# A bias table written out 128 times and moved to GpSimd's queue, in a hybrid mixer and MoE block

## The chip, the cores and the metric

The kernel runs on one core of one Trainium2 chip. The metric is the device time of one execution in microseconds (us). All numbers of this kernel are 32-bit; matrices are multiplied in a split form (below) so that TensorE can take them in its fast 32-bit form.

## What is computed

One layer on 512 tokens of width 1024: a mixer of three branches, then a mixture of 16 experts, each with a residual. Shortened to what this case touches:

```python
def chunked_rel_attention(q, k, v, rel_bias):          # 8 heads of 64, chunks of 64
    scores = einsum('bcqhd,bckhd->bhcqk', q, k_band) * (A_HEAD_DIM ** -0.5)
    rel = clip(q_pos[:, None] - k_pos[None, :], -REL_CLIP, REL_CLIP) + REL_CLIP   # REL_CLIP = 128
    bias = rel_bias[:, rel]                             # rel_bias: 8 heads x 257
    scores = where(valid, scores + bias, -1e30)
    return einsum('bhcqk,bckhd->bcqhd', softmax(scores), v_band)

def reference(x, ...):
    xn = rms_norm(x, norm1_g)
    x = x + hybrid_mixer(xn, w_in, ..., w_branch, w_out)   # attention, spatial gating, linear recurrence
    xn = rms_norm(x, norm2_g)
    x = x + hierarchical_moe(xn, ..., w_gate, w_up, w_down)  # 16 experts, two per token
    return rms_norm(x, final_norm_g)
```

The bias of a query and a key depends on their distance alone, so the 128 x 256 bias tile of a head is a Toeplitz matrix: each row is the row above moved by one.

## The kernel before

It is written engine by engine, with semaphores by hand. Weights come in blocks of 512 KB (128 partitions x 1024 values), numbered b. A block goes through four hands in this order:

- SyncE (SP) loads block b into `raw` slot b % 4 (`load`, line 373). It first waits until block b - 4, the slot's last owner, has had its low part made.
- ScalarE (ACT) copies it to `w_hi` in the reduced form (`split_hi`, line 332), three blocks ahead of TensorE (`AHEAD = 3`), after block b - 4 has been multiplied.
- GpSimd (POOL) subtracts to get `w_lo` (`split_lo`, line 344) for all blocks of the mixer.
- TensorE (PE) multiplies hi by hi, hi by lo and lo by hi (`three`, lines 947 to 949). Before block b it waits for that block's low part (`lo_wait`).

Blocks 0 to 3 are the weights of the gating branch's second half (`B_SV`), 4 to 7 those of attention's v (`B_V`), from 8 on come the head pairs (`B_PAIR`), from 28 the gates, from 64 the output matrix. Then come the experts, 12 blocks each, with 24 buffers (`raw_a`, `raw_c`, `raw`, `raw_mg`, `macc`, `xn2T`) and the low parts made by VectorE.

At the start ACT squares the four row tiles of x, POOL takes the reciprocal root (line 530), VectorE (DVE) normalises a tile (line 1277), PE turns it (line 958), ACT writes `xn_hi` (line 653) and DVE `xn_lo` (`x_lo`, line 1267). In program order POOL then makes the low parts of blocks 0, 1, 2, clears `raw` slot 4 (line 535, semaphore `zero_done`, for which SP waits before it loads block 8), and goes on with block 3.

The bias: `rel_bias` is loaded into 8 partitions of `probs`, one per head. DVE repeats the last value 127 times behind the 257 (line 1256, early), ACT's queue stores the 8 rows of 384 values in the DRAM tensor `toep` (line 647, 12 KB), and SP's queue reads `toep` into `bias` (line 411): partition p takes 256 values from offset 1 + p, so all 128 partitions read overlapping pieces of the same 8 rows. The tile that arises is mirrored; DVE reads it backwards (`bias_and_max`, lines 1341 and 1343). POOL masks a corner of it (line 541) and the spatial weights (line 544) after the low part of block 8. The first reader of `bias` is the attention of the first head pair, after block 12.

Tiles are laid out in SBUF by hand with pads: `to_512` (96 values per partition) ahead of `raw`, `to_line` (8 values) ahead of `xT_hi`, and 5 values more than needed in `xrT`.

Of the kernel before, what the change touches and what calls it, by code (L numbers as in the profile page):

```python
# [22 lines left out]
F32 = mybir.dt.float32  # L23
# [3 lines left out]
ALU = mybir.AluOpType  # L27
ACT = mybir.ActivationFunctionType
AX = mybir.AxisListType

P = 128
TOK = 512
# [62 lines left out]
def build(nc, a, out):  # L95

    slots = nc.dram_tensor("slots", [SLOT_TILES * P, D], F32, kind="Internal").ap()
    toep = nc.dram_tensor("toep", [HEADS, 3 * P], F32, kind="Internal").ap()
# [7 lines left out]
    with ctx:  # L106
# [10 lines left out]
        sb(ctx, "to_512", [P, 96])  # L117
# [30 lines left out]
        with ExitStack() as s1:  # L148
# [14 lines left out]
            xrT = sb(s1, "xrT", [P, CONV + 4 + TOK])  # L163
# [6 lines left out]
            sb(s1, "pad_b1", [P, AREA_B - (NT * AW + 4 * P + 4 * P + AW + 2 * NPAIR * P + CONV + 4 + 7 * TOK)])  # L170
# [6 lines left out]
        with ExitStack() as s2:  # L177
# [15 lines left out]
            sb(s2, "to_line", [P, 8])  # L193
# [32 lines left out]
        def y_hi(t):  # L226
# [10 lines left out]
            "g1_in chan_in diag_in sgu_in relb_in toep_filled toep_out bias_in bias_done route_in g2_in "  # L237
# [126 lines left out]
        def _(sp):  # L364
# [43 lines left out]
            for kp in range(4):  # L408
                load(B_V + kp, rows2(w_in, 2 * kp, V0), 2)
            sp.wait_ge(S["toep_out"], 16)  # L410
            sp.dma_start(bias[:, :, :], bass.AP(toep.tensor, 1, [[1, P], [3 * P, HEADS], [1, 2 * P]]))\
              .then_inc(S["bias_in"], 16)
# [106 lines left out]
        def _(pool):  # L519
# [14 lines left out]

            pool.memset(gate_buf[:, 0:2, :], 0.0).then_inc(S["zero_done"], 1)
            for b in range(AHEAD, B_PAIR + AHEAD):
                split_lo(pool, b)
                if b == B_PAIR:

                    pool.wait_ge(S["bias_in"], 16)  # L540
                    pool.memset(bias[0:CHUNK, :, 0:CHUNK], NEG).then_inc(S["bias_done"], 1)
# [92 lines left out]
        def _(act):  # L634

            act.dma_start(g1_rows[:, :], a["norm1_g"][0:1, :].broadcast_to([P, D])).then_inc(S["g1_in"], 16)
            act.dma_start(probs[0:HEADS, 0, 0:2 * CLIP + 1], a["rel_bias"][0]).then_inc(S["relb_in"], 16)
# [7 lines left out]

            act.wait_ge(S["toep_filled"], 1)
            act.dma_start(toep, probs[0:HEADS, 0, 0:3 * P]).then_inc(S["toep_out"], 16)
# [69 lines left out]
            for j in range(NPAIR):  # L717
                for r in range(PER_PAIR):
# [6 lines left out]
                    if r == KK:  # L725

                        if j > 0:
                            act.wait_ge(S["conv_done"], j)
                        take(b - 1, xrT[:, CONV - 1:CONV - 1 + TOK], ACT.Copy)
# [513 lines left out]
        def _(dve):  # L1243
            chained = [0]

            def link(ins):
# [8 lines left out]
            dve.wait_ge(S["relb_in"], 16)  # L1255
            dve.tensor_copy(probs[0:HEADS, 0, 2 * CLIP + 1:3 * P],
                            probs[0:HEADS, 0, 2 * CLIP:2 * CLIP + 1].to_broadcast([HEADS, P - 1]))\
               .then_inc(S["toep_filled"], 1)
# [21 lines left out]
            for t in range(NT):  # L1280
                x_lo(t)

            dve.wait_ge(S["sguT_ps"], 1)
# [46 lines left out]
            def bias_and_max(n):  # L1330
# [9 lines left out]
                if w > near:  # L1340
                    link(dve.tensor_scalar(dst[:, 0:w - near], ps[:, 4 + buf, 0:w - near], DH ** -0.5,
                                           bias[:, h, 2 * P - 1:2 * P], ALU.mult, ALU.add))
# [408 lines left out]
```

## Time and profile before

| | us |
|---|---|
| median of 3 runs | 869.15 |
| lowest and highest | 867.15 and 870.6 |
| the profiled execution, whole | 869.15 |
| its span, first to last instruction | 867.4 |
| mean granted TensorE clock | 0.965 |
| PE busy | 801.0 |
| DVE, ACT, POOL busy | 495.5, 449.2, 218.0 |

The profiled execution's own time is also the median, so its durations can be used as they stand; 1.75 us of it lie outside the span. The rows are shown in a section of their own below: a row of a timeline is an instruction or a run of them, with its start, its length, and in brackets how long the engine stood idle before it and what ended that. A run of several (x3) starts with the first and ends with the last.

### The profile page before, as it was taken

The numbers are of one execution on the slowest core, as the hardware profiler recorded it, in microseconds if no ns is written. First come the engines' busy times: TensorE is split into PE (matmuls) and PEld (weight loads), VectorE is DVE, ScalarE is ACT, GpSimd is POOL, SyncE is SP. The second block draws the span as 40 slices with busy tenths as digits, with TensorE's granted clock in tenths as the row PEclk, the third lists the DMA queues.
The fourth block names the chain that finished last, engine by engine and source line by source line (L and its number), as shares of the span: only waits on it lengthen the run. The fifth ranks groups of instructions, "written<-read, shape, count | busy, mean of one in ns | idle before, by whom it ended". The sixth has DMA issues, their size and how long they took to land.

```text
span 867.4 us, 10612 instructions
## 1 busy us (share of the span) xinstructions
PE 801.0 (92%) x3635; PEld 631.7 (73%) x3635; DVE 495.5 (57%) x649; ACT 449.2 (52%) x580; POOL 218.0 (25%) x126
## 2 busy tenths in 40 slices
PE   4999999999979999999999967899999999999960
PEld 3887766676756888888888866688787787877750
DVE  6613647657472222204012435698889898988865
ACT  5244637454552232323222221687888878887842
POOL 5554323132232344444444234000000000000013
PEclk9999999999999999999999967999999999999995
DMA  8665451512120343333328364999999999975945
GB/s 308 179 243 188 128 194 49 194 49 74 40 80 27 89 169 118 99 93 95 98 96 280 131 239 197 366 400 385 405 389 393 408 395 406 389 299 209 367 137 207
DMA packets 126633, 186.76 MB, mean 215 GB/s; under 512 B 9149, under 2 KB 61957, under 8 KB 126597
## 3 DMA queue, kind: packets, MB, share of 16 engines
q1 hardware_dynamic: 119156, 167.82, 54.3%
q10 hardware_dynamic: 5136, 10.08, 3.1%
q0 software_dynamic: 2304, 8.39, 2.7%
q8 instruction: 22, 0.36, 0.2%
q14 instruction: 15, 0.11, 0.0%
HBM read 158.99 MB, written 27.28 MB: 215 GB/s over the span
## 4 chain that ended last, share of the span: by engine, by line
PE 81%; DVE 7%; ACT 4%; issue 3%; DMA 2%; POOL 1%; ACTq 1%; DVEq 0%; SPq 0%
PE ps L947 24%; PE ps L949 23%; PE ps L948 23%; PE ps L1030 3%; PE ps L1010 2%; PE ps L1171 2%; PE ps L1019 1%; DVE w_lo L350 1%; PE ps L1119 1%; ACT w_hi L339 1%; DVE rgate L1394 1%; PE ps L1178 1%; DMA x<-in_x 1%; ACT xn L879 1%; DMA slots<-y_tile 1%
## 5 line engine op out<-in xcount | busy, mean ns | idle before, releaser
L344 POOL TENSOR_TENSOR w_lo<-raw,w_hi 128x1024 fp32r<-128x1024 f32 x72 | 176.2, 2450 | 286.8 <-ACT w_hi L332 286.8
L332 ACT ACTIVATE w_hi<-raw 128x1024 fp32r<-128x1024 f32 x73 | 77.0, 1057 | 169.0 <-PE ps L949 159.9
L947 PE MATMUL ps<-xn_hi,w_hi 128*128 128x512 f32 x352 | 143.8, 409 | 0.0
L949 PE MATMUL ps<-xn_hi,w_lo 128*128 128x512 f32 x352 | 137.5, 390 | 0.0
L948 PE MATMUL ps<-xn_lo,w_hi 128*128 128x512 f32 x352 | 137.3, 390 | 0.0
L947 PE MATMUL ps<-w_hi,xT_hi 128*128 128x512 f32 x256 | 105.2, 411 | 8.1 <-DVE xT_lo L1644 5.5
L948 PE MATMUL ps<-w_lo,xT_hi 128*128 128x512 f32 x256 | 102.3, 399 | 0.0
L949 PE MATMUL ps<-w_hi,xT_lo 128*128 128x512 f32 x256 | 102.2, 399 | 0.0
L947 PEld LDWEIGHTS ps<-xn_hi,w_hi 128*128 128x128 f32 x352 | 66.0, 188 | 26.8 <-issue 13.8
L614 POOL DMA_INDIRECT raw_mg<-slots,slot_idx x7 | 6.9, 982 | 303.6 <-ACTq L930 295.1
L949 PEld LDWEIGHTS ps<-xn_hi,w_lo 128*128 128x128 f32 x352 | 66.1, 188 | 14.4
L948 PEld LDWEIGHTS ps<-xn_lo,w_hi 128*128 128x128 f32 x352 | 66.2, 188 | 13.1 <-issue 1.0
L350 DVE TENSOR_TENSOR w_lo<-raw_mg,w_hi 128x1024 fp32r<-128x1024 f32 x57 | 68.0, 1221 | 4.3 <-ACT w_hi L339 1.7
L947 PEld LDWEIGHTS ps<-w_hi,xT_hi 128*128 128x128 f32 x256 | 48.9, 191 | 24.2 <-DVE w_lo L350 8.0
L1457 DVE SCALAR_TENSOR_TENSOR macc<-raw,ps 128x512 f32<-128x512 f32 x16 | 11.0, 688 | 96.5 <-PE ps L949 96.3
L339 ACT ACTIVATE w_hi<-raw_mg 128x1024 fp32r<-128x1024 f32 x57 | 59.7, 1056 | 11.3 <-PE ps L949 11.3
L350 DVE TENSOR_TENSOR w_lo<-raw,w_hi 128x1024 fp32r<-128x1024 f32 x43 | 51.3, 1220 | 14.6 <-ACT w_hi L339 14.6
L949 PEld LDWEIGHTS ps<-w_hi,xT_lo 128*128 128x128 f32 x256 | 48.9, 191 | 11.7
L948 PEld LDWEIGHTS ps<-w_lo,xT_hi 128*128 128x128 f32 x256 | 48.9, 191 | 10.4
L947 PE MATMUL ps<-w_hi,hT_hi 128*128 128x512 f32 x128 | 51.8, 405 | 2.9 <-DVE hT_lo L1651 2.9
L339 ACT ACTIVATE w_hi<-raw 128x1024 fp32r<-128x1024 f32 x43 | 44.0, 1055 | 16.1 <-PE ps L949 16.1
L949 PE MATMUL ps<-w_hi,hT_lo 128*128 128x512 f32 x128 | 50.5, 395 | 0.0
(260 smaller groups left out, 1457.5 us busy)
## 6 DMA issues: line engine op xcount, KB each, us to landing
raw<-in_w_in SPq DMA_DIRECT2D x52, 512.0 KB, 3.7
raw_mg<-in_exp_w_down SPq DMA_DIRECT2D x36, 512.0 KB, 8.3
raw<-in_exp_w_gate SPq DMA_DIRECT2D x28, 512.0 KB, 10.3
raw_a<-in_exp_w_gate SPq DMA_DIRECT2D x27, 512.0 KB, 9.8
raw_c<-in_exp_w_up SPq DMA_DIRECT2D x27, 512.0 KB, 9.2
slots<-raw SPq DMA_DIRECT2D x24, 512.0 KB, 6.5
raw_mg<-in_exp_w_up SPq DMA_DIRECT2D x21, 512.0 KB, 9.8
raw<-in_exp_w_up SPq DMA_DIRECT2D x16, 512.0 KB, 9.5
```

The source lines that it names most:

```text
L332: nc.scalar.activation(w_hi[:, b % HI_SLOTS, :], raw_buf(b), ACT.Copy)\
L339: nc.scalar.activation(w_hi[:, (8 + r) % HI_SLOTS, :], buf, ACT.Copy).then_inc(S["hi_act"], 1)
L344: eng.tensor_tensor(w_lo[:, b % HI_SLOTS, :], raw_buf(b), w_hi[:, b % HI_SLOTS, :].bitcast(F32), ALU.subtract)\
L350: eng.tensor_tensor(w_lo[:, (8 + r) % HI_SLOTS, :], place(at, r)[0], w_hi[:, (8 + r) % HI_SLOTS, :].bitcast(F32), ALU.subtract)\
L879: act.activation(at.y, ps[:, 5:7, :].rearrange("p a n -> p (a n)"), ACT.Copy).then_inc(S["y_act"], 1)
L947: pe.matmul(dst, hi_l, hi_r, start=start, stop=False)
L948: pe.matmul(dst, hi_l, lo_r, start=False, stop=False)
L949: return pe.matmul(dst, lo_l, hi_r, start=False, stop=stop)
L1010: pe.matmul(ps[:, 4 + n % 2, 0:(i + 1) * P], qT[hp, jp % 2, i * P:(i + 1) * P], kT[hp, jp % 2, 0:(i + 1) * P], start=True, stop=True).then ...
L1030: mm = pe.matmul(ps[DH * h:DH * (h + 1), 7, i * P:(i + 1) * P], v_rows[:, kt, (2 * jp + h) * DH:(2 * jp + h + 1) * DH], probsT[:, kt * P:( ...
L1171: mm = pe.transpose(ps[:, 3 + k // 4, (k % 4) * P:(k % 4 + 1) * P], rows[:, k * P:(k + 1) * P], ident[:, :])
L1457: dve.scalar_tensor_tensor(out=macc[:, 1, :], in0=gate_buf[:, g % 3, :], scalar=1.0, in1=ps[:, 2 + c, :], op0=ALU.add, op1=ALU.mult)\
```

## The change

- `toep` grows from 8 x 384 to 8 x 128 x 384 values: every head's row is stored 128 times, one copy per partition (1.57 MB instead of 12 KB). Each partition then reads its 256 values out of its own copy, from offset 127 - p, so that the tile arrives the right way round.
- `rel_bias` is loaded next to the row that is built; DVE writes the row in two copies, the repeated value first, and the 257 values reversed. This stands behind the four `x_lo` now, not ahead of the normalisation, and the load of `bias` is not issued by SP, nor the store of `toep` by ACT: POOL issues both, after the low part of block 2, and waits for the first to land before the second.
- POOL waits for `bias` and masks after block 4, not block 8.
- DVE makes `xn_lo` of tile 0 behind the normalisation of tile 2 and that of tile 1 behind that of tile 3, not all four at the end.
- The pads `to_512` and `to_line` go, and `xrT` is 515 values, not 520. Since tiles begin at multiples of 32 bytes, `xrT` still takes as much room as before.

GpSimd's program from the reciprocal roots on, before (`w_lo` are the low parts of blocks 0, 1, ...; `raw` the cleared slot):

```order
L530 TENSOR_TENSOR stat<-stat,minus_half 128x1 [waits x0_stat] x3
L344 TENSOR_TENSOR w_lo<-raw,w_hi 128x1024 [waits hi_act] x3
L535 MEMSET raw 128x1024
L344 TENSOR_TENSOR w_lo<-raw,w_hi 128x1024 [waits hi_act] x6
L541 MEMSET bias 64x8x64 [waits bias_in]
L544 AFFINE_SELECT sgu_wT<-sgu_wT 128x512 [waits sguT_done]
```

The same place in the changed kernel:

```order
L525 TENSOR_TENSOR stat<-stat,minus_half 128x1 [waits x0_stat] x3
L342 TENSOR_TENSOR w_lo<-raw,w_hi 128x1024 [waits hi_act] x3
L532 DMA toep<-probs 1024x1x384 [waits toep_rev]
L534 DMA bias<-toep 128x8x256 [waits toep_out]
L537 MEMSET raw 128x1024
L342 TENSOR_TENSOR w_lo<-raw,w_hi 128x1024 [waits hi_act] x2
L543 MEMSET bias 64x8x64 [waits bias_in]
L546 AFFINE_SELECT sgu_wT<-sgu_wT 128x512 [waits sguT_done]
```

Two DMAs, each with a wait, now stand between the low parts of blocks 2 and 3, and the wait for `bias` stands after two more low parts, not six.

VectorE's program at the start, before (`x` is the row tile that is normalised, `probs` holds the bias row):

```order
L1256 COPY probs<-probs 8x127 [waits relb_in]
L1262 TENSOR_SCALAR stat<-stat 128x1 [waits x0_sq_done,g1_in]
L1262 TENSOR_SCALAR stat<-stat 128x1 [waits x0_sq_done]
L1277 SCALAR_TENSOR_TENSOR x<-x,stat,g_rows 128x1024 [waits x0_rstd]
L1262 TENSOR_SCALAR stat<-stat 128x1 [waits x0_sq_done]
L1277 SCALAR_TENSOR_TENSOR x<-x,stat,g_rows 128x1024 [waits x0_rstd]
L1262 TENSOR_SCALAR stat<-stat 128x1 [waits x0_sq_done]
L1277 SCALAR_TENSOR_TENSOR x<-x,stat,g_rows 128x1024 [waits x0_rstd] x2
L1267 TENSOR_TENSOR xn_lo<-ps,xn_hi 128x8x128 [waits xn_hi_done] x4
L1284 COPY par<-ps 128x56 [waits sguT_ps]
```

and in the changed kernel, from the normalisation of tile 1 on:

```order
L1257 TENSOR_SCALAR stat<-stat 128x1 [waits x0_sq_done]
L1272 SCALAR_TENSOR_TENSOR x<-x,stat,g_rows 128x1024 [waits x0_rstd]
L1257 TENSOR_SCALAR stat<-stat 128x1 [waits x0_sq_done]
L1272 SCALAR_TENSOR_TENSOR x<-x,stat,g_rows 128x1024 [waits x0_rstd]
L1262 TENSOR_TENSOR xn_lo<-ps,xn_hi 128x8x128 [waits xn_hi_done]
L1272 SCALAR_TENSOR_TENSOR x<-x,stat,g_rows 128x1024 [waits x0_rstd]
L1262 TENSOR_TENSOR xn_lo<-ps,xn_hi 128x8x128 [waits xn_hi_done] x3
L1281 COPY probs<-probs 8x127 [waits relb_in]
L1284 COPY probs<-probs 8x257
L1287 COPY par<-ps 128x56 [waits sguT_ps]
```

The copy that fills the bias row went from ahead of the normalisation to behind the last `xn_lo`, and one `xn_lo` went ahead of the last normalised tile. On SyncE's queue the load of `bias` between block 7 and block 8 is gone; the rest stands as it was.

The diff, without the renaming of `toep_filled` to `toep_rev` in the list of semaphores:

```diff
-    toep = nc.dram_tensor("toep", [HEADS, 3 * P], F32, kind="Internal").ap()
+    toep = nc.dram_tensor("toep", [HEADS, P, 3 * P], F32, kind="Internal").ap()
...
-        sb(ctx, "to_512", [P, 96])
...
-            xrT = sb(s1, "xrT", [P, CONV + 4 + TOK])
+            xrT = sb(s1, "xrT", [P, CONV - 1 + TOK])
...
-            sb(s2, "to_line", [P, 8])
... SyncE
-            sp.wait_ge(S["toep_out"], 16)
-            sp.dma_start(bias[:, :, :], bass.AP(toep.tensor, 1, [[1, P], [3 * P, HEADS], [1, 2 * P]]))\
-              .then_inc(S["bias_in"], 16)
... GpSimd
+            pool.wait_ge(S["toep_rev"], 2)
+            pool.dma_start(toep, probs[0:HEADS, 0, 0:3 * P].unsqueeze(1).to_broadcast([HEADS, P, 3 * P])).then_inc(S["toep_out"], 16)
+            pool.wait_ge(S["toep_out"], 16)
+            pool.dma_start(bias[:, :, :], bass.AP(toep.tensor, P - 1, [[3 * P - 1, P], [3 * P * P, HEADS], [1, 2 * P]]))\
+                .then_inc(S["bias_in"], 16)
+
             pool.memset(gate_buf[:, 0:2, :], 0.0).then_inc(S["zero_done"], 1)
             for b in range(AHEAD, B_PAIR + AHEAD):
                 split_lo(pool, b)
-                if b == B_PAIR:
+                if b == AHEAD + 1:
                     pool.wait_ge(S["bias_in"], 16)
-                    pool.memset(bias[0:CHUNK, :, 0:CHUNK], NEG).then_inc(S["bias_done"], 1)
+                    pool.memset(bias[0:CHUNK, :, 3 * CHUNK:4 * CHUNK], NEG).then_inc(S["bias_done"], 1)
... ScalarE
-            act.dma_start(probs[0:HEADS, 0, 0:2 * CLIP + 1], a["rel_bias"][0]).then_inc(S["relb_in"], 16)
+            act.dma_start(probs[0:HEADS, 1, 0:2 * CLIP + 1], a["rel_bias"][0]).then_inc(S["relb_in"], 16)
...
-            act.wait_ge(S["toep_filled"], 1)
-            act.dma_start(toep, probs[0:HEADS, 0, 0:3 * P]).then_inc(S["toep_out"], 16)
... VectorE
-            dve.wait_ge(S["relb_in"], 16)
-            dve.tensor_copy(probs[0:HEADS, 0, 2 * CLIP + 1:3 * P],
-                            probs[0:HEADS, 0, 2 * CLIP:2 * CLIP + 1].to_broadcast([HEADS, P - 1]))\
-               .then_inc(S["toep_filled"], 1)
...
                    .then_inc(S["x0_norm"], 1)
-            for t in range(NT):
+                if t >= 2:
+                    x_lo(t - 2)
+            for t in range(NT - 2, NT):
                 x_lo(t)
+            dve.wait_ge(S["relb_in"], 16)
+            dve.tensor_copy(probs[0:HEADS, 0, 0:P - 1],
+                            probs[0:HEADS, 1, 2 * CLIP:2 * CLIP + 1].to_broadcast([HEADS, P - 1]))\
+               .then_inc(S["toep_rev"], 1)
+            dve.tensor_copy(probs[0:HEADS, 0, P - 1:3 * P], probs[0:HEADS, 1, 2 * CLIP::-1])\
+               .then_inc(S["toep_rev"], 1)
...
-                                           bias[:, h, 2 * P - 1:2 * P], ALU.mult, ALU.add))
+                                           bias[:, h, 0:1], ALU.mult, ALU.add))
...
-                                              scalar=DH ** -0.5, in1=bias[:, h, near - 1::-1],
+                                              scalar=DH ** -0.5, in1=bias[:, h, 2 * P - near:],
```

## Rows read from the trace of the kernel before

**Rows 1.** The page: engines, granted clock in 40 slices, chain by engine

```profile
PE 801.0 (92%) x3635; PEld 631.7 (73%) x3635; DVE 495.5 (57%) x649; ACT 449.2 (52%) x580; POOL 218.0 (25%) x126
PEclk9999999999999999999999967999999999999995
PE 81%; DVE 7%; ACT 4%; issue 3%; DMA 2%; POOL 1%; ACTq 1%; DVEq 0%; SPq 0%
```

**Rows 2.** Waits of PE, whole span: us in total, times, longest

```profile
PE ps L958 <- DVE x L1277: 12.2, 2, 10.3
...
PE ps L947 <- POOL w_lo L344: 3.0, 1, 3.0
```

**Rows 3.** Timeline of POOL, 7 to 36 us: start, length, engine, line, operation

```profile
12.03 1.52 POOL L530 TENSOR_TENSOR stat<-stat,minus_half 128x1 f32<-128x1 f32 x1 [0.95 <-DVE stat L1262]
13.52 8.05 POOL L344 TENSOR_TENSOR w_lo<-raw,w_hi 128x1024 fp32r<-128x1024 f32 x3
21.51 0.96 POOL L535 MEMSET raw<- 128x1024 f32 x1
27.25 7.12 POOL L344 TENSOR_TENSOR w_lo<-raw,w_hi 128x1024 fp32r<-128x1024 f32 x3 [4.78 <-ACT w_hi L332]
```

**Rows 4.** Timeline of DVE, first 25 us

```profile
6.20 0.21 DVE L1256 COPY probs<-probs 8x127 f32<-8x127 f32 x1 [4.12 <-DMA probs<-in_rel_bias]
...
13.59 3.38 DVE L1277 SCALAR_TENSOR_TENSOR x<-x,stat,g_rows 128x1024 f32<-128x1024 f32 x1 [0.44 <-POOL stat L530]
16.89 4.61 DVE L1267 TENSOR_TENSOR xn_lo<-ps,xn_hi 128x1024 fp32r<-128x1024 f32 x4
```

**Rows 5.** Timeline of PE, 17 to 36 us: last turned tile, block 0, start of block 3

```profile
17.02 1.09 PE L958 MATMUL ps<-ident,x 128*128 128x128 f32 x8 [1.85 <-DVE x L1277]
18.25 0.47 PE L947 MATMUL ps<-w_hi,xn_hi 128*128 128x512 f32 x1
...
35.23 0.39 PE L949 MATMUL ps<-w_hi,xn_lo 128*128 128x512 f32 x1
35.46 0.39 PE L947 MATMUL ps<-w_hi,xn_hi 128*128 128x512 f32 x1
```

**Rows 6.** Timeline of ACT and SyncE's queue, 30 to 50 us

```profile
46.60 1.06 ACT L332 ACTIVATE w_hi<-raw 128x1024 fp32r<-128x1024 f32 x1 [2.47 <-PE ps L949]
...
32.10 18.43 SPq L373 DMA_DIRECT2D raw<-in_w_in  x5
```

**Rows 7.** DMA issues: KB each, median us to landing; then the GpSimd-issued kind

```profile
raw_a<-in_exp_w_gate SPq DMA_DIRECT2D x27, 512.0 KB, 9.8
raw_c<-in_exp_w_up SPq DMA_DIRECT2D x27, 512.0 KB, 9.2
...
out<-raw_mg SPq DMA_DIRECT2D x4, 512.0 KB, 2.6
...
bias<-toep SPq DMA_DIRECT2D x1, 1024.0 KB, 6.4
...
L587 POOL DMA_INDIRECT slots<-xn,slot_idx x8 | 7.9, 986 | 13.3 <-DVE slot_idx L1614 11.1 <-issue 2.1
```

**Rows 8.** Busy time by stretch; last three numbers granted clock, DMA share, GB/s

```profile
8.00:12.00 4.00, 1.70 (x8) 1.63 (x9) 2.85 (x6) 3.66 (x7) 2.28 (x3) 1.00 1.04 409
...
24.00:28.00 4.00, 4.00 (x21) 3.34 (x22) 2.73 (x10) 1.99 (x3) 0.76 (x1) 1.00 0.17 62
...
600.00:700.00 100.00, 99.10 (x459) 79.74 (x458) 88.57 (x83) 80.70 (x88) 0.00 (x0) 1.00 1.04 400
```

**Rows 9.** Timeline of PE after two gaps, and the stretch when the clock returns

```profile
257.85 0.77 PE L947 MATMUL ps<-br_hi,w_hi 128*128 128x512 f32 x1 [2.97 <-POOL w_lo L344]
258.41 0.63 PE L948 MATMUL ps<-br_lo,w_hi 128*128 128x512 f32 x1
...
258.84 0.63 PE L949 MATMUL ps<-br_hi,w_lo 128*128 128x512 f32 x1
...
263.00:264.00 1.00, 1.00 (x6) 0.77 (x6) 0.00 (x0) 0.00 (x0) 0.00 (x0) 0.65 0.00 0
...
536.82 0.80 PE L947 MATMUL ps<-w_hi,xT_hi 128*128 128x512 f32 x1 [2.68 <-DVE xT_lo L1644]
```

**Rows 10.** Waits of SyncE's queue, 540 to 830 us, and the chain's tile pitch

```profile
SPq L377 <- DVE w_lo L350: 93.0, 108, 2.9
...
603.46 0.87 PE ps L1171 x8
...
640.36 0.87 PE ps L1171 x8
```

**Rows 11.** Readers of bias: duration ns min/median/max, first and last start

```profile
L1343 DVE SCALAR_TENSOR_TENSOR probs<-ps,bias x22: 276/424/426, 96.8 to 271.6; 128x256 f32<-128x256 f32 x16, 128x128 f32<-128x128 f32 x6
L1341 DVE TENSOR_SCALAR probs<-ps,bias x11: 345/471/485, 103.9 to 271.1; 128x256 f32<-128x256 f32 x6, 128x128 f32<-128x128 f32 x5
```

More of the change, by code:

```diff
@@ L169, in build @@
             gu = sb(s1, "gu", [P, TOK])
-            sb(s1, "pad_b1", [P, AREA_B - (NT * AW + 4 * P + 4 * P + AW + 2 * NPAIR * P + CONV + 4 + 7 * TOK)])
+            sb(s1, "pad_b1", [P, AREA_B - (NT * AW + 4 * P + 4 * P + AW + 2 * NPAIR * P + CONV - 1 + 7 * TOK)])
             br_hi = sb(s1, "br_hi", [P, 3, NPAIR, TOK], F32R)
@@ L236, in build @@
             "ident_done consts_pool consts_dve zero_done zeros_stored "
-            "g1_in chan_in diag_in sgu_in relb_in toep_filled toep_out bias_in bias_done route_in g2_in "
+            "g1_in chan_in diag_in sgu_in relb_in toep_rev toep_out bias_in bias_done route_in g2_in "
             "sgu_raw sguT_ps sguT_done mask_done sv_sq sv_stat sv_rstd sv_done sp_exp sp_done halved "
@@ L728, in _ @@
                             act.wait_ge(S["conv_done"], j)
-                        take(b - 1, xrT[:, CONV - 1:CONV - 1 + TOK], ACT.Copy)
+                        take(b - 1, xrT[:, CONV - 1:], ACT.Copy)
                     if r == QQ:
```

## The prediction, as put on record

> **What bounds the kernel now.** I read the page's first lines, then PE's waits, then the timelines of the first 50 us, since the change lives there. The page shows PE busy for 801.0 of 867.4 us, its clock at the full level in nearly all slices, and 81% of the chain on PE [rows 1]. PE's longest wait is for the first normalised tile, 12.2 us in two pieces; for POOL's low parts it waits once, 3.0 us [rows 2]. From 18.25 us on PE runs block after block without a gap: a matmul starts every 0.23 us, and block 3 begins at 35.46 [rows 5]. So anything that holds PE in this stretch is added to the end in full, and anything taken from another engine here is worth nothing. The number to watch is the margin of block 3's low part: POOL makes those of blocks 3, 4, 5 from 27.25 on, 7.12 us for three, the first done near 29.6 [rows 3]. PE needs it at 35.46. The margin is 5.8 us.
>
> **The store and the load on POOL.** This is the heavy edit. Of block 3 onward every low part is POOL's, and two DMAs with two waits now stand ahead of it. The sum runs along POOL:
>
> - Start. The third low part ends at 21.5 [rows 3]. VectorE must first write the reversed row: its four xn_lo end at 21.5 before [rows 4]. In the change the first comes earlier, so the last ends near 20.4 (16.97 + 3 x 1.15). The first copy took 0.21 [rows 4]; the second, 257 values from SBUF, is at most the 0.42 of a 256-value read of `bias` [rows 11]. DVE's last normalisation took 3.38 us beside POOL's low part, where the rest of that form take about 1.3, so I let the copies start only as POOL stops: ready at 21.5 + 0.6 = 22.1.
> - X, from issue to landing of the store: 8 x 128 x 1536 bytes = 1.57 MB. No row shows a large transfer out of 8 partitions. Low end: the full rate of 409 GB/s [rows 8] gives 3.9 us, and 1.3 us on top, which is what the 2.6 us of a 512 KB store [rows 7] leaves over its 1.3 us at that rate: 5.2. High end: a full transfer takes 1/16 of its bytes from 8 partitions; were that share their limit, 25.6 GB/s, it would be 61.5 + 1.3 = 62.8. I take twice that share, 51 GB/s: 30.8 + 1.3 = 32.1. It is a choice nearer the high end, since all rows I have at high rates spread over 128 partitions and here a single row of 1.5 KB is read 128 times over. Little else is on the queues: 62 GB/s from 24 to 28 us [rows 8].
> - G, the time that POOL itself spends on issuing the second DMA (1024 pieces of 1 KB). A GpSimd-issued DMA of 128 pieces keeps POOL for 0.99 us [rows 7]. Low end: the same, 1.0. High end: eight times that, 7.9. I take the middle, 4.4. The first DMA's issue overlaps its own transfer and lies inside X.
> - Then the clearing of `raw`, 0.96, and the low part, 2.40 (7.12 / 3) [rows 3].
>
> Block 3's low part is ready at 22.1 + X + G + 3.4 = 25.5 + X + G, and PE stands still for X + G - 10.0 us. With 32.1 + 4.4 that is **26.5 us**. With both low ends it is negative (-3.8): hidden. With both high ends 60.7.
>
> The Trainium skill has a price where no row does: "SBUF — State Buffer", section on the DMA port swizzle, gives 27.6 GB/s for a transfer over partitions 0 to 3 and about 27 GB/s per port; 0 to 7 reach two ports. By that page the store would take an estimated 29 us and about 2 more, and the wait of PE would be about 25. No run here shows it.
>
> **What starts again after the gap.** After 2.97 us without work PE's matmuls came 0.43 us apart, not 0.23, the clock at 1.2 GHz, from 257.85 until inside 263 to 264 [rows 8, 9]: 12 matmuls x 0.2 = 2.4, with the small ones 2.9. After the 2.68 us gap at 536.82 [rows 9] it was eight matmuls, 1.6. I take 2.3. POOL then needs 2.4 us per block and PE 5.4, so the other low parts do not delay PE again. POOL's wait for `bias` stands after block 4's: the load took 6.4 from issue [rows 7], and G + 0.96 + 2 x 2.40 cover all but a fraction; block 5 is wanted 10.9 us after block 3. SyncE's loads wait for low parts: block 7's goes out after block 3's part, block 8's after block 4's and `zero_done`. Before, block 8's load went at 32.10 and its high part was made at 46.60, when PE let it [rows 6]; the 14 us between stay, as both ends move together.
>
> **Small edits.** `xn_lo` of tile 0 came 16.89 to 18.05, and PE began block 0 at 18.25, 0.14 after the last turned tile (17.02 + 1.09) [rows 4, 5]. With tile 0's part made before, at most 0.2 us is gained; the last normalisation waits for POOL's low part until 15.7 anyway and does not move. I count -0.1. SyncE and ACT lose one DMA issue each; neither is waited for there. DVE's read of `bias` forwards in place of backwards: 424 ns for 256 columns and 276 for 128 is 1.16 ns per column backwards, the forward form beside it 485 and 345, 1.09 [rows 11]: at most 0.02 us each in 32 readers, nothing.
>
> **The pads.** All tiles move down by 384 bytes, and those behind `router_b` and from `br_hi` on start 32 bytes past a multiple of 64. Two places could feel it. The expert loads: `raw_a`, `raw` and `raw_mg` go from multiples of 256 bytes to 128 past one, where `raw_c` stood before; it landed in 9.2 us, `raw_a` in 9.8 [rows 7], so this offset showed no price. Were the transfers some per cent slower, the demand of 400 GB/s against the best of 409 [rows 8] would no longer be met, but two tiles take 36.9 us [rows 10] and the buffers hold two tiles: a load landing in 10 us has 26 us to spare, and SyncE's queue waits 93.0 us in all for buffers [rows 10], not buffers for it. I count 0. PE reading `xn_hi`, `xn_lo` and `br_*` at the new offset: no row shows it at this rate; between 0 and, as an estimate, one line more in 32 on 0.23 us for the mixer's some 1500 matmuls, 11 us. I take 0, because PE's pace was the same for all tiles before.
>
> **Sum.** 26.5 + 2.3 - 0.1 = +28.7 on the span of 867.4, so 896.1, and with the 1.75 us outside it **897.9 us**. The profiled execution, 869.15, is also the median, so nothing is corrected.
>
> **Rivals.**
>
> - *The store is limited by engines, not by the partitions.* Eight source rows may keep half the 16 DMA engines busy: 204 GB/s, 7.7 + 1.3 = 9.0 us. For it: a load of 1024 pieces out of eight rows, `bias` itself, landed 1 MB in 6.4 us [rows 7]. Against: that read DRAM, not 8 partitions. PE waits 9.0 + 4.4 - 10.0 = 3.4, and with the clock's 1.6 to 2.9 the time is 874.6; with the first issue taking 7.9 before the transfer and G at 7.9, 886. The Trainium skill, "DMA: Bandwidth & Descriptors", on how many engines a DMA uses, has a rule that gives 8 here, as the largest number up to 16 that divides both slowest dimensions, 8 and 1024. Chance 0.22.
> - *Hidden: not slower.* The store and the second issue together stay under 10.0 us, which is where this decides; X of 5.2 with G of up to 4.8 does it. The margin swallows both, and the time is 869.1. For it: a 512 KB store landed in 2.6. Against: it needs the full rate from 8 partitions. Chance 0.07.
> - *One share only.* X near 62.8: PE waits 57.2, the time is 928.6. Chance 0.07.
> - *The offsets cost too.* The forecast's wait plus up to 11 us of slower matmuls or loads: 903 to 909. It decides if PE's spacing leaves 0.227 in blocks 0 to 2. Chance 0.07.
>
> **How the numbers follow.** The forecast has the rest, 0.57, with its own range from 885 (X of 20, G of 4) to 912 (X of 42, G of 7.9). A gain of over 0.5% would need 4.3 us, and nothing in the change is worth more than 0.2: 0.02. A measurement of this kernel can tell about 0.5% from no change. Within 0.5% (864.8 to 873.5) lie the hidden case and the shortest of the eight-engine case: 0.10. Slower: 0.88. The range reaches from 873 to 915 and leaves out the one-share case, the hidden one and little else.
>
> **What would show it.** On POOL between the third and the fourth low part: one DMA, a wait of X for `toep` (32 us forecast, 9 in the first rival), a second DMA of G, the clearing, and a PE gap before block 3 equal to X + G - 10.0, with matmuls 0.43 us apart behind it. The bytes per us over the wait tell 51 from 204 GB/s. The expert stage should take the same time as before, and blocks 0 to 2 the same spacing. The prediction is wrong if PE has no gap at block 3, if the gap is there but a later wait was absorbed by it, or if the time is lost behind 100 us.

## The result, and the profile after

The changed kernel is slower: its median is 904.01 us against 869.88 us of the kernel before, run beside it on the same chip, a ratio of 1.0396 with the interval [1.0359, 1.0433]. The span of the profiled execution grew from 867.4 to 900.3 us, by 32.9; by the medians the whole time grew by 34.1. The forecast was 897.9 us.

The page of the changed kernel, with its line of busy times, the granted clock in 40 slices and the chain by engine (to be held against [rows 1]):

```profile
PE 811.4 (90%) x3635; PEld 631.8 (70%) x3635; DVE 488.2 (54%) x650; ACT 449.1 (50%) x580; POOL 220.1 (24%) x128
...
PEclk9859999999999999999999995999999999999995
...
PE 78%; DVE 6%; DMA 6%; ACT 4%; issue 3%; POOL 1%; ACTq 1%; SPq 0%; DVEq 0%
```

Two things are to be seen. DMA's share of the chain went from 2% to 6%. And PE, whose work is the same, is busy for 10.4 us longer. PE's waits of the changed kernel (against [rows 2]):

```profile
PE ps L946 <- POOL w_lo L342: 27.6, 2, 24.7
```

GpSimd's timeline of the changed kernel at the place of [rows 3]:

```profile
13.57 8.07 POOL L342 TENSOR_TENSOR w_lo<-raw,w_hi 128x1024 fp32r<-128x1024 f32 x3
22.23 1.34 POOL L532 DMA_DIRECT2D toep<-probs  x1 [0.59 <-DVE probs L1284]
56.13 0.98 POOL L534 DMA_DIRECT2D bias<-toep  x1 [32.56 <-DMA toep<-probs]
57.10 0.97 POOL L537 MEMSET raw<- 128x1024 f32 x1
58.02 4.66 POOL L342 TENSOR_TENSOR w_lo<-raw,w_hi 128x1024 fp32r<-128x1024 f32 x2
```

The store goes out at 22.23, GpSimd stands for 32.56 us until it has landed, issues the load in 0.98, and only then clears `raw` and makes block 3's low part. The two DMAs, issue to landing, and the rate from 26 to 56 us (last number of the row, GB/s; the third last is the granted clock):

```profile
toep<-probs POOLq DMA_DIRECT2D x1, 1536.0 KB, 33.6
...
bias<-toep POOLq DMA_DIRECT2D x1, 1024.0 KB, 6.1
```

```profile
26.00:56.00 30.00, 9.76 (x42) 7.52 (x40) 4.66 (x29) 4.06 (x5) 0.00 (x0) 0.72 0.47 50
```

TensorE's timeline of the changed kernel at block 3:

```profile
60.42 0.80 PE L946 MATMUL ps<-w_hi,xn_hi 128*128 128x512 f32 x1 [24.66 <-POOL w_lo L342]
61.01 0.63 PE L947 MATMUL ps<-w_lo,xn_hi 128*128 128x512 f32 x1
...
66.13 0.52 PE L947 MATMUL ps<-w_lo,xn_hi 128*128 128x512 f32 x1
66.49 0.39 PE L948 MATMUL ps<-w_hi,xn_lo 128*128 128x512 f32 x1
```

It idles for 24.66 us, and the matmuls behind the gap come 0.43 us apart, the pace at 1.2 GHz, until 66.13: 13 of them, 13 x 0.2 = 2.6 us. That explains 24.6 (27.6 - 3.0) + 2.6 = 27.2 of the 32.9 us. The remaining 5.7 are no gap. It shows where the same matmuls of the two kernels are laid side by side. Durations by tile (ns, lowest, median and highest, then first and last start), before:

```profile
L948 PE MATMUL ps<-xn_lo,w_hi x352: 387/389/402, 62.9 to 449.3; 128*128 128x512 f32 x176
L949 PE MATMUL ps<-w_hi,xT_lo x256: 390/393/628, 537.8 to 825.1; 128*128 128x512 f32 x128
L949 PE MATMUL ps<-w_hi,mg_lo x64: 389/389/395, 455.6 to 502.0; 128*128 128x512 f32 x64
```

and after:

```profile
L947 PE MATMUL ps<-xn_lo,w_hi x352: 389/394/398, 91.5 to 483.0; 128*128 128x512 f32 x176
L948 PE MATMUL ps<-w_hi,xT_lo x256: 388/397/632, 570.7 to 858.2; 128*128 128x512 f32 x128
L948 PE MATMUL ps<-w_hi,mg_lo x64: 389/389/395, 489.5 to 535.9; 128*128 128x512 f32 x64
```

The end of a matmul is modelled, so these durations are soft, and the pace is better read from the starts: the 352 matmuls on `xn_lo` spread over 386.4 us before and 391.5 after. The mean step from one start to the next, within an unbroken run of matmuls at the full clock, went from 0.2278 to 0.2332 us for all matmuls on `xn`, from 0.2328 to 0.2342 for those on `xT`, and stayed at 0.227 for those on `mg`. So the two tiles that look alike by their durations do not weigh the same: on `xn` the pace lost 5.4 ns per matmul, on `xT`, which was slow before the change already, 1.4 ns. TensorE's timeline of the changed kernel in block 0 has the same sign: of these two starts the second is that of the 24th matmul, and after a first step of 0.32 come 22 steps of 0.233, which in the kernel before are 0.227.

```profile
17.93 0.48 PE L946 MATMUL ps<-w_hi,xn_hi 128*128 128x512 f32 x1
...
23.37 0.40 PE L948 MATMUL ps<-w_hi,xn_lo 128*128 128x512 f32 x1
```

So the pads, which I had counted at nothing, are the second cause.

### The profile page after: what moved, and what is told of

Its sections match the earlier page's. It is cut to its first block, busy times and chain, and to the rows that moved or that the text cites. A ratio compares the mean times of both kernels' runs of the same rounds, so it can differ in the third digit from the quotient of the medians.

```text
span 900.3 us, 10613 instructions
## 1 busy us (share of the span) xinstructions
PE 811.4 (90%) x3635; PEld 631.8 (70%) x3635; DVE 488.2 (54%) x650; ACT 449.1 (50%) x580; POOL 220.1 (24%) x128
## 4 chain that ended last, share of the span: by engine, by line
PE 78%; DVE 6%; DMA 6%; ACT 4%; issue 3%; POOL 1%; ACTq 1%; SPq 0%; DVEq 0%
PE ps L946 23%; PE ps L948 22%; PE ps L947 22%; DMA toep<-probs 4%; PE ps L1029 2%; PE ps L1009 2%; PE ps L1170 1%; PE ps L1018 1%; DVE w_lo L348 1%; PE ps L1118 1%; PE ps L1193 1%; DMA raw<-in_w_in 1%; ACT w_hi L337 1%; DVE rgate L1397 1%; PE ps L1177 1%
## 5 line engine op out<-in xcount | busy, mean ns | idle before, releaser
L948 PEld LDWEIGHTS ps<-w_hi,xT_lo 128*128 128x128 f32 x256 | 48.6, 190 | 11.9
L947 PEld LDWEIGHTS ps<-w_lo,xT_hi 128*128 128x128 f32 x256 | 48.7, 190 | 10.4
L947 PE MATMUL ps<-w_lo,hT_hi 128*128 128x512 f32 x128 | 51.4, 402 | 0.0
```

The source lines that it names most:

```text
L947: pe.matmul(dst, hi_l, lo_r, start=False, stop=False)
L948: return pe.matmul(dst, lo_l, hi_r, start=False, stop=stop)
```

## The experiments

Line numbers shift by a few from kernel to kernel; the names of tiles don't. "The old pads" are `to_512` of 96 values, `to_line` of 8 and `xrT` of 520. My theory from here on: the store leaves over the few ways out that its 8 partitions have and GpSimd waits for it (some 27 us), and the pads cost the rest. "Way out" stands for whatever it is that neighbouring partitions have in common when a DMA reads them. The rivals are given with each run.

**The pads alone.** The kernel before with the three pad edits and nothing else:

```diff
-        sb(ctx, "to_512", [P, 96])
-            xrT = sb(s1, "xrT", [P, CONV + 4 + TOK])
+            xrT = sb(s1, "xrT", [P, CONV - 1 + TOK])
-            sb(s2, "to_line", [P, 8])
```

> The kernel before, with only the three pads changed as in the change. Of the 32.9 us by which the span grew, 24.7 are the gap at block 3 and about 2.8 the half clock behind it; some 5 to 6 us are left. Theory A (the matmuls that read xn, br, xT or hT at 32 bytes past a multiple of 64 start 0.233 us apart, not 0.227): +5 to +8 us on the kernel before, with mean durations of 394 to 396 ns in place of 389 in the gate stage and none at the output matrix, whose operands stay at multiples of 64. Theory B (the offsets cost nothing, the rest comes from loads that run against the bias table): within 1 us of the kernel before.

It took 876.46 us against 870.76, ratio 1.0062 [1.0039, 1.0086]: 5.7 us, with an interval from 3.4 to 7.5. Its matmuls on `xn_lo` take 394 ns, as in the changed kernel.

**All but the pads.** The changed kernel with the old pads:

> The changed kernel with the three pads as they were before. Theory A: faster than the changed kernel by 5 to 8 us, 28 us over the kernel before, with the gap at block 3 unchanged at 24.7 us. Theory B: as slow as the changed kernel, 34 us over.

It took 898.73 us against 870.76, ratio 1.0304 [1.0276, 1.0331]. 28.0 and 5.7 make 33.7, where the whole change cost 34.1: the two parts add up within the intervals. PE's gap at block 3 was 23.4 us here, not quite the 24.7 that I expected.

**The table in one copy.** The changed kernel with the old pads, where `toep` is 8 x 384 again and read as before; order, queues and waits are those of the change:

```diff
-    toep = nc.dram_tensor("toep", [HEADS, P, 3 * P], F32, kind="Internal").ap()
+    toep = nc.dram_tensor("toep", [HEADS, 3 * P], F32, kind="Internal").ap()
-            pool.dma_start(toep, probs[0:HEADS, 0, 0:3 * P].unsqueeze(1).to_broadcast([HEADS, P, 3 * P]))
+            pool.dma_start(toep, probs[0:HEADS, 0, 0:3 * P])
```

> The order and the queues of the change (both DMAs on GpSimd, waits included, late bias row), the old pads, but the table stored once per head (12 KB) and read mirrored as before. Theory A (the 1.57 MB out of 8 partitions make the wait): the store lands in 2 to 3 us, block 3's low part is ready before 35.5, no gap, within 1 us of the kernel before. Theory B (a GpSimd-issued DMA with two waits is slow whatever its size): a gap of 5 us and more at block 3 and a time 6 us or more over.

It took 871.82 us against 870.76, ratio 1.0011 [0.9991, 1.0031]. GpSimd's timeline of this kernel:

```profile
25.71 0.98 POOL L536 DMA_DIRECT2D bias<-toep  x1 [2.80 <-DMA toep<-probs]
```

The same two DMAs with the same two waits, in the same place, cost nothing that can be measured while the store has 12 KB: it lands in 3.2 us, and the margin of block 3 covers it. Neither the move to GpSimd nor the issue of the load's 1024 pieces is the cause, but the transfer.

**The same bytes from other partitions.** The changed kernel with the old pads, the eight source rows in partitions 0, 4, ..., 28 in place of 0 to 7 (the rows between hold zeros and are written along):

```diff
-            pool.dma_start(toep, probs[0:HEADS, 0, 0:3 * P].unsqueeze(1).to_broadcast([HEADS, P, 3 * P]))
+            pool.dma_start(toep, probs[0:4 * HEADS:4, 0, 0:3 * P].unsqueeze(1).to_broadcast([HEADS, P, 3 * P]))
```

> The change with the old pads, and the eight source rows in partitions 0, 4, 8 ... 28 in place of 0 to 7; the bytes, the pieces and the queue are the same. Theory A (neighbouring partitions share a way out, about 26 GB/s for four of them): the store lands in 9 us, not 33.6, and the gap at block 3 is 0 to 1 us; time 0 to 2 us over the kernel before. Theory B (a single row of 1.5 KB read 128 times, or the writes to DRAM, limit it): 33 us to landing and the gap of 24.7 us stay.

It took 872.84 us against 870.76, ratio 1.0028 [1.0007, 1.005]. The store and GpSimd's wait in this kernel:

```profile
toep<-probs POOLq DMA_DIRECT2D x1, 1536.0 KB, 10.5
...
33.13 0.98 POOL L536 DMA_DIRECT2D bias<-toep  x1 [9.49 <-DMA toep<-probs]
```

Bytes, pieces, engine and queue are the same; only the partitions differ, and 33.4 us (the store with the old pads) become 10.5. Less the 3.2 us that a store of 12 KB takes, that is 30.2 against 7.3 us, a factor of 4.1: 52 GB/s from partitions 0 to 7, 215 GB/s from eight that lie four apart. So neighbouring partitions share a way out of SBUF, and this is what bounds the store from partitions 0 to 7. PE's gap shrinks to 2.02 us, somewhat more than the 0 to 1 expected, since the store took 10.5 us and not 9.

That the other partitions merely brought more DMA engines into play can be ruled out. The stretches of both kernels in which the store ran almost alone, first the changed kernel, then this one (last two numbers: share of the 16 DMA engines that was busy, GB/s):

```profile
30.00:40.00 10.00, 5.76 (x25) 4.31 (x23) 1.38 (x10) 2.12 (x2) 0.00 (x0) 0.95 0.48 51
```

```profile
28.00:32.00 4.00, 4.00 (x19) 3.34 (x18) 3.00 (x20) 1.06 (x1) 0.00 (x0) 1.00 0.51 210
```

About half of the 16 engines' time was busy in both, and together they moved four times as much in the second. The factor of four alone does not say how many neighbours share a way: with groups of four, partitions 0 to 7 reach two ways and 0, 4, ..., 28 eight; with groups of eight it would be one and four. No run here separates the two. The Trainium skill has a number for it in "SBUF — State Buffer", section on the DMA port swizzle: four neighbouring partitions share a port of some 27 GB/s. By it, partitions 0 to 7 reach two ports and 0, 4, ..., 28 eight, 54 and 216 GB/s as an estimate; the trace agrees with both rates, 52 and 215, at a source that is one row read over and over, and so with groups of four.

**The store on ScalarE's queue.** As the changed kernel with the old pads, but the store is issued by ACT, where it stood before:

```diff
-            pool.dma_start(toep, probs[0:HEADS, 0, 0:3 * P].unsqueeze(1).to_broadcast([HEADS, P, 3 * P])).then_inc(S["toep_out"], 16)
+            act.wait_ge(S["toep_rev"], 2)
+            act.dma_start(toep, probs[0:HEADS, 0, 0:3 * P].unsqueeze(1).to_broadcast([HEADS, P, 3 * P])).then_inc(S["toep_out"], 16)
```

> The change with the old pads and the 1.57 MB store issued by ScalarE's queue, out of the same 8 partitions; GpSimd still waits for it and issues the load. If the 8 partitions set the time, it lands in about 33 us again and the gap at block 3 stays near 24 us. If GpSimd's way of issuing sets it, it lands in 10 us or less and the gap is gone.

It took 896.45 us against 871.05, ratio 1.0293 [1.0273, 1.0314]. GpSimd still waited 33.41 us for the store, and PE's gap was 22.5 us. Who issues it makes little difference (25.4 us over the kernel before here, 28.0 with GpSimd's issue; this one is a median of two runs only); from where it reads does.

**Don't wait at once.** If the cost is GpSimd standing still, it should vanish when the wait stands later. The changed kernel with the old pads, the store as it is, the wait and the load behind block 8's low part, the mask two blocks later:

```diff
-            pool.wait_ge(S["toep_out"], 16)
-            pool.dma_start(bias[:, :, :], bass.AP(toep.tensor, P - 1, [[3 * P - 1, P], [3 * P * P, HEADS], [1, 2 * P]]))
...
+                if b == B_PAIR:
+                    pool.wait_ge(S["toep_out"], 16)
+                    pool.dma_start(bias[:, :, :], bass.AP(toep.tensor, P - 1, [[3 * P - 1, P], [3 * P * P, HEADS], [1, 2 * P]]))
+                if b == B_PAIR + 2:
```

> The changed kernel with the old pads; GpSimd still issues the large store of toep behind the low part of block 2, but waits for it and loads bias only behind the low part of block 8, and masks two blocks later. The store takes its 33 us in the shade. Theory A (what costs is only that the low parts of blocks 3, 4, 5 stand behind the wait): the store lands near 56, GpSimd reaches block 8 well after that, no gap of PE at block 3, low parts of blocks 3 to 7 in time, bias ready near 110 us or before its first reader, time within 0.5% of the kernel before (868 to 875). Rival B (a slow store of 1.5 MB over few ways also slows the weight loads beside it): PE waits for low parts or high parts of blocks 8 to 12, the time is 880 or more. Rival C (bias comes too late for the first head pair): VectorE waits for it near 97 us and PE behind it, 3 to 10 us more.

It took 882.57 us against 870.22, ratio 1.0135 [1.0113, 1.0157]. My theory as I had written it for this run failed: the gap at block 3 is gone, and 12 us are lost all the same. First two pieces of the chain of waits (start, length, what), then ScalarE's and TensorE's timelines of this kernel:

```profile
29.41 27.16 DMA raw<-in_w_in
...
62.90 10.54 DMA bias<-toep
```

```profile
56.59 1.06 ACT L332 ACTIVATE w_hi<-raw 128x1024 fp32r<-128x1024 f32 x1 [20.09 <-DMA raw<-in_w_in]
```

```profile
60.13 0.80 PE L948 MATMUL ps<-w_hi,xn_hi 128*128 128x512 f32 x1 [3.02 <-POOL w_lo L344]
...
90.48 2.07 PE L1061 MATMUL ps<-conv,wa_diag 128*128 128x512 f32 x2 [6.90 <-DVE conv L1387]
```

The stretch while the store ran, 30 to 56 us (last three numbers: clock, DMA share, GB/s):

```profile
30.00:56.00 26.00, 26.00 (x116) 21.56 (x115) 9.47 (x23) 2.12 (x2) 6.49 (x3) 1.00 0.59 93
```

A weight load that went out at 29.41 landed after 27.16 us, just as the store ended. The store's own rate is 1.57 MB / 34.1 us = 46 GB/s, so 47 are left for the weights, where a load may get over 400 [rows 8]. The Trainium skill, "DMA: Bandwidth & Descriptors", section on queues, rings and completion order, has each DMA engine take turns between its queues packet by packet; that the weights got about as much as the store fits it, but the turns were not looked at, so no run here tests it. Three us of gap come from this. The other 6.90 are the old mechanism in a new place: the load of `bias` goes out at 62.90, takes 10.54 us beside the delayed weight loads, GpSimd waits for it ahead of the reciprocal roots that VectorE wants for `sv_rows`, VectorE then begins `conv` at 85, and PE waits for that. The two gaps make 9.9 of the 12 us. Both are followed by matmuls at the lower clock (granted clock 0.92 from 60 to 80 us and 0.83 from 80 to 100), which fits the rest. So such a slow store is not free, even where nobody waits for it: it holds back what shares the DMA engines with it.

**Which pad.** Each of the three edits alone, in the kernel before:

> The kernel before with xrT of 515 values and the pad behind it grown to match, which moves br_hi, br_lo, xn_hi and xn_lo by 32 bytes and nothing else that matters. Theory A: the matmuls of the mixer with xn and br are 0.233 us apart in place of 0.227; where PE sets the pace that is 8 blocks, 36 blocks of gates and branches, some 1000 matmuls: +5 to +6 us. Theory B: nothing.

> The kernel before without the pad of 8 values ahead of xT_hi: xT, hT, y_tile and raw_c start at 32 past a multiple of 64, all else stays. Theory A: hT's and xT's matmuls go from 393 to 397 ns, 0.3 us per tile at most, +1 to +3 us over 17 tiles. Theory B: nothing.

> The kernel before without the pad of 96 values: every tile moves down by 384 bytes, so all keep their place to a multiple of 128, and lose a multiple of 256 or 512. Theory A (only the multiple of 64 matters to TensorE, and the loads have room): within 0.5 us of the kernel before. Theory B (loads into raw at 128 past a multiple of 256 are slower): longer landing in the expert stage and some us more.

- `xrT` of 515: 874.93 us against 871.05, ratio 1.0037 [1.0023, 1.0051]. It moves `br_*` and `xn_*` by 32 bytes. The cost, 2.0 to 4.4 us, is less than the 5 to 6 expected.
- `to_line` gone: 870.91 us, ratio 0.9995 [0.9981, 1.0009]. It moves `xT_*` and `hT_*` by 32 bytes; their matmuls take 397 to 398 ns in place of 393 to 395, yet no difference of time can be measured (-1.7 to +0.8 us), where I expected 1 to 3. The row of `xT_lo` in this kernel is below; why so little comes of it is seen from the starts, further down.
- `to_512` gone: 870.44 us, ratio 0.9998 [0.9986, 1.0011]. All tiles move by 384 bytes, no duration changes. The loads of the experts do not mind these addresses: `raw_mg` landed after 8.5 us here and 8.3 before, `raw` after 10.0 and 10.3.

Taken singly the three make 3.2 us by the medians, all together 5.7; the intervals are wide enough for both to be true, so this is no sign that they act on each other, nor is it excluded.

```profile
L948 PE MATMUL ps<-w_hi,xT_lo x256: 391/397/628, 540.4 to 828.9; 128*128 128x512 f32 x128
```

**A coarser multiple for xT.** The matmuls of the experts took 393 to 395 ns in the kernel before, those of the mixer 389. `xT_hi` lay 128 bytes past a multiple of 256, `xn_hi` on one. The kernel before with two edits:

```diff
-            sb(s2, "to_line", [P, 8])
+            sb(s2, "to_line", [P, 40])
...
-            for t in range(NT):
+                if t >= 2:
+                    x_lo(t - 2)
+            for t in range(NT - 2, NT):
```

> The kernel before with two small edits: xn_lo of tiles 0 and 1 are made between the normalisations, as in the change, and the pad ahead of xT_hi has 40 values, so that xT_hi starts at a multiple of 256 bytes instead of 64. It asks whether the 4 ns by which matmuls on xT and hT are longer than those on xn (393 to 389 ns) come from the address. Theory A (a coarser multiple helps): medians 389, 770 matmuls x 3 x some 4 ns, the two expert tiles take 36.6 instead of 36.9 us, time 865 to 868. Rival B (64 bytes is all that counts): medians stay 392 to 397, time as before within 0.3%. The order of xn_lo is worth 0 to 0.2 us by both.

It took 866.87 us against 870.22, ratio 0.9948 [0.9931, 0.9966]: the one kernel here that beats the kernel before. The same line as above, in this kernel, and two of the chain's tile turns, two tiles apart:

```profile
L949 PE MATMUL ps<-w_hi,xT_lo x256: 388/389/628, 539.6 to 823.4; 128*128 128x512 f32 x128
```

```profile
586.56 0.88 PE ps L1171 x8
...
623.00 0.87 PE ps L1171 x8
```

Two tiles take 36.44 us in place of 36.9 [rows 10]; for the sixteen tiles, eight pairs, that makes some 3.7 us, against 3.4 measured by the medians (3.0 to 6.0 by the interval of the ratio). The new order of `xn_lo` shows no gain of its own: block 0 began at 18.59 here, at 18.25 before [rows 5].

**Which operand.** In all runs so far only the activations moved against the weights. The kernel before with the weight blocks `w_hi` and `w_lo` moved by 32 bytes and all other tiles at the multiple they had (the values come out of `to_512`):

```diff
-        sb(ctx, "to_512", [P, 96])
+        sb(ctx, "to_512", [P, 32])
+        sb(ctx, "w_off", [P, 8])
         w_hi = sb(ctx, "w_hi", [P, HI_SLOTS, 1024], F32R)
         w_lo = sb(ctx, "w_lo", [P, HI_SLOTS, 1024], F32R)
+        sb(ctx, "back_on", [P, 56])
```

> The kernel before with w_hi and w_lo, the weight blocks, moved to 32 bytes past a multiple of 64, and all other tiles at the multiple they had. Theory A (any operand of a matmul at such an offset makes it longer, moving or stationary): matmuls on xn, br and mg take 393 to 397 ns instead of 389, and those on xT and hT of the mixture's w_hi blocks too, time above the kernel before by 5 to 9 us. Rival B (it is the tile that is moved with 512 columns alone, or the activations alone): only the head pairs and branches, where w_hi is the moving operand, or none at all, show the longer time, 0 to 4 us.

It took 877.43 us against 870.22, ratio 1.0083 [1.0062, 1.0104]. Now `mg_lo` is slow too:

```profile
L951 PE MATMUL ps<-w_hi,mg_lo x64: 392/396/397, 462.4 to 510.0; 128*128 128x512 f32 x64
```

**Address or distance.** Two readings were left: a tile off a multiple of 64 bytes is slow, or two operands are slow when they are out of step with each other. The kernel before with everything moved by 32 bytes, weights and activations alike:

```diff
-        sb(ctx, "to_512", [P, 96])
+        sb(ctx, "to_512", [P, 88])
```

> The kernel before with to_512 at 88 values in place of 96: every tile behind it, weights and activations alike, starts 32 bytes lower. The runs so far can be read in two ways, since wherever a matmul grew longer, its two operands had also moved against each other. Theory A (the address itself counts: a tile that starts off a multiple of 64 is read more slowly): matmuls on xn, br, mg, xT and hT all take 394 to 398 ns, time 6 to 10 us above the kernel before (876 to 881). Rival B (the distance between the two operands counts: 389 ns where w_hi and the activations agree in their address modulo 256, 393 where they are 128 apart, 394 to 398 where they are 32 or 96 apart): medians as before, 389 for xn, br, mg and 392 to 393 for xT and hT, time within 0.3% of the kernel before.

It took 873.34 us against 870.73, ratio 1.0017 [0.9993, 1.004]. The rows in this kernel:

```profile
L948 PE MATMUL ps<-xn_lo,w_hi x352: 387/389/632, 64.4 to 452.3; 128*128 128x512 f32 x176
L949 PE MATMUL ps<-w_hi,xT_lo x256: 390/393/628, 542.3 to 830.4; 128*128 128x512 f32 x128
```

All durations are as before, though no operand of these matmuls starts on a multiple of 64 any more. It is the distance. The median time is 2.6 us up, which the interval does not tell from nothing; the profiled execution is 4.6 us longer in its span at a granted clock of 0.958 against 0.965. With the addresses modulo 256, the matmuls of all kernels fall in one table (the tile's address less that of `w_hi`, whichever of the two is the stationary one). The last column is the mean step from start to start at the full clock:

| distance, bytes modulo 256 | seen at | median duration, ns | mean step, us |
|---|---|---|---|
| 0 | xn, br, mg before; mg after; xT, hT with `to_line` of 40; xn, br, mg with all moved | 389 | 0.2267 to 0.2279 |
| 128 | xT, hT before, with `to_512` gone, and with all moved | 392 to 395 | 0.2326 to 0.2329 |
| 32 to either side | xn, br after and with `xrT` of 515; xn, br, mg with the weights moved | 394 to 396 | 0.2332 to 0.2333 |
| 96 | xT, hT after, with `to_line` gone and with the weights moved | 395 to 398 | 0.2340 to 0.2343 |

The steps of the experts' stage, 21 of them between the two starts of each kernel: the kernel before (128), without `to_line` (96), and with `to_line` of 40 (0).

```profile
616.84 0.39 PE L949 MATMUL ps<-w_hi,xT_lo 128*128 128x512 f32 x1
...
621.72 0.39 PE L949 MATMUL ps<-w_hi,xT_lo 128*128 128x512 f32 x1
```

```profile
619.74 0.39 PE L948 MATMUL ps<-w_hi,xT_lo 128*128 128x512 f32 x1
...
624.65 0.39 PE L948 MATMUL ps<-w_hi,xT_lo 128*128 128x512 f32 x1
```

```profile
617.83 0.39 PE L949 MATMUL ps<-w_hi,xT_lo 128*128 128x512 f32 x1
...
622.61 0.39 PE L949 MATMUL ps<-w_hi,xT_lo 128*128 128x512 f32 x1
```

That is 4.88, 4.91 and 4.78 us. By the pace there is one good case, distance 0, and all others lie within 2 ns of each other; the durations hide this. One thing the runs leave open is the period. In every kernel and for every operand of the first line, the distance is an odd multiple of 256 bytes, never a multiple of 512. That 0 modulo 512 is as good is therefore not shown.

**From pace to time.** What the steps cost, and what the clock gives back, as an estimate: steps counted in the trace times their growth, and the granted clock of all runs of a kernel and of the kernel before beside it, as (1 - clock) x span, the time that stretches at half speed cost. This counts stretches in which PE stands idle too, so it is rough.

| kernel | by the steps, us | by the clock, us | sum | measured by medians, interval |
|---|---|---|---|---|
| three pads gone | +9.4 | -4.6 (0.962 to 0.968) | +4.8 | +5.7, 3.4 to 7.5 |
| `xrT` of 515 | +7.8 | -6.0 (0.963 to 0.970) | +1.8 | +3.9, 2.0 to 4.4 |
| weights moved | +10.4 | -4.2 (0.964 to 0.969) | +6.2 | +7.2, 5.4 to 9.1 |
| `to_line` gone | +1.5 | -0.5 (0.963 to 0.964) | +1.0 | -0.1, -1.7 to +0.8 |
| `to_line` of 40 | -5.3 | +0.7 (0.964 to 0.963) | -4.6 | -3.4, -6.0 to -3.0 |

So a slower pace of the mixer's matmuls came with a higher granted clock in all three kernels that had it, and by this estimate 4 to 6 us of the 8 to 10 lost came back. Why the clock was higher, no run shows.

## Why the prediction came out, and where it was off

- **The mechanism and its place** were right: one DMA, a wait, a second DMA, the clearing, and a gap of PE ahead of block 3. The formula for the gap, X + G - 10.0, gives 33.6 + 0.98 - 10.0 = 24.6 with the measured terms; the trace has 24.66.
- **VectorE's row ready** at 22.1: the store was issued at 22.23.
- **X**, chosen at 32.1 between 5.2 and 62.8: 33.6. I chose twice the share that 8 partitions have in a full transfer, near the high end for lack of a row. No row decided between once and twice, so that this came out so close is in part luck. The run with the source rows four apart shows what sets it, the partitions that are read: the same bytes took 10.5 us.
- **G**, chosen at 4.4 between 1.0 and 7.9: 0.98, the low end. I took the middle where a single row had a price, 0.99 us for a DMA of 128 pieces. Eight times the pieces cost GpSimd the same; the rule of taking the nearest row would have been better. This is the largest miss within the forecast's own case: the forecast had 3.4 us too many here.
- **The lower clock**, 2.3: 2.6, 13 matmuls.
- **Nothing later delays PE**: right. PE's only other wait for GpSimd is again some 3.0 us (27.6 less 24.7), and the low parts of blocks 4 and 5 were in time. `bias` landed 6.1 us after its issue and was masked before anyone asked.
- **Small edits**, -0.1: no gain can be told. The first matmul of block 0 started at 17.93, before at 18.25 [rows 5], but in the other kernels with the new order of `xn_lo` it started anywhere from 17.9 to 18.7.
- **The pads**, taken at 0 between 0 and 11: 5.7. Here the reasoning failed, not just a size. I wrote that PE's pace was the same for all tiles before. It was not: the steps were 0.2278 us on `xn` and 0.2328 on `xT` (389 and 393 ns by the medians shown above), in the trace I had, and a tile-by-tile look would have shown that something differs between tiles. The bound of 11 us rested on one line more in 32, which no row and no run shows; the step on `xn` grew by 5.4 ns in 228, less than that. The rival "the offsets cost too", with 903 to 909 and a chance of 0.07, is the one that came true on top of the forecast; its sign, a spacing that leaves 0.227 in blocks 0 to 2, is there: 22 matmuls from 18.25 to 23.37 are 0.233 apart. The expert loads, the other half of that term, cost no time, but they did not stay as they were. `raw_mg` before and after:

```profile
raw_mg<-in_exp_w_down SPq DMA_DIRECT2D x36, 512.0 KB, 8.3
```

```profile
raw_mg<-in_exp_w_down SPq DMA_DIRECT2D x36, 512.0 KB, 12.0
```

  With the pads alone it is 11.9, with everything moved by 32 bytes 12.2, and with each pad edit alone 8.3 to 8.8. PE's wait for VectorE's low parts is the same before and after (2.6 and 2.5 us), so the buffers covered it; SyncE's wait for them fell from 93.0 to 54.0 us, so the margin shrank. Which addresses do this is open.
- **The sum**: 26.5 + 2.3 - 0.1 = 28.7 was forecast for the span. Measured: 24.6 + 2.6 leave 5.7 of the 32.9, and the pads alone, in their own run, cost 5.7. G too high by 3.4 and the pads too low by 5.7 cancelled in part, so that the total, 34.1 by the medians against 28.7, looks better than its terms.
- **The eight-engine rival** was right in that about half of the 16 engines' time was busy (0.48), and wrong in that this set the time: they moved 51 GB/s, not 204. With the rows four apart, at 210 GB/s, the eight ways and the half of the engines would bound the store alike, and no run tells them apart.

## What to carry to other kernels

Before a DMA reads or writes a few partitions only, look how closely these lie together: eight rows in partitions 0 to 7 moved 52 GB/s, the same eight spread four apart 215. A slow transfer costs twice, once to who waits for it and once to the loads beside it, so moving the wait away is not enough. And lay the two operands of a hot matmul at the same address modulo 256 bytes; a pad of 32 values was worth 3.4 us here, and an innocent shortening of a tile cost about as much. To find such a thing, compare the steps between starts tile by tile, not the durations.

## What I had not expected of the hardware

- The pace of matmuls with 512 columns of 32-bit data depends on the distance of its two operands in SBUF: one starts every 0.227 to 0.228 us when they agree modulo 256 bytes, every 0.2326 to 0.2343 at the three other distances seen. It is the same whether weights or activations are moved. Why, no run shows; that both are read at the same time is only a guess.
- Durations mislead here. By their medians, the experts' matmuls lose 4 ns without `to_line` and gain 4 ns with `to_line` of 40 values. Their stretch went from 287.3 us (537.8 to 825.1) to 288.5 in the one case and to 283.8 in the other. The steps say the same as the stretch: 1.4 ns slower, 5 ns faster.
- The issue of a DMA keeps GpSimd for 0.75 us (12 KB store), 0.98 (1024 pieces of 1 KB) and 1.34 (1024 pieces of 1.5 KB, repeated from 8 rows): pieces cost it little.
- Small VectorE operations grow long beside GpSimd. Of the kernel before and of the changed kernel, VectorE's timeline:

```profile
27.27 2.40 DVE L1303 TENSOR_TENSOR chan<-chan 128x4 f32<-128x4 f32 x1
29.70 2.33 DVE L1304 TENSOR_SCALAR chan<-chan 128x4 f32<-128x4 f32 x1
```

```profile
27.09 0.16 DVE L1306 TENSOR_TENSOR chan<-chan 128x4 f32<-128x4 f32 x1
27.29 0.17 DVE L1307 TENSOR_SCALAR chan<-chan 128x4 f32<-128x4 f32 x1
```

Before, GpSimd made low parts from 27.25 to 34.4 [rows 3], and such an operation of four values per partition took as long as one low part; in the changed kernel GpSimd stood still, and it took 0.16. VectorE was done with this work at 31.7 us in place of 40.5. That was worth nothing, since PE waited for none of it.
